# Half of the first sixteen modulation vectors by TensorE, transposed tokens in four PSUM banks in turn

## The reference

```
mod = silu(c) @ w_mod + b_mod              # 6 * 1024 numbers
sh1, sc1, g1, sh2, sc2, g2 = split(mod, 6)
u = layer_norm(x) * (1 + sc1) + sh1        # 512 x 1024
z = u @ w_in                               # q, k, v, f, ca, cb, ga, gb
...
```

## Time and profile before

| | us |
|---|---|
| median of three executions | 1709.74 |
| the profiled execution, whole | 1707.66 |
| its span in the profile | 1705.8 |
| TensorE (PE) busy | 1616.3 (95%) |
| VectorE (DVE) busy | 1320.6 (77%) |
| ScalarE (ACT) busy | 689.8 (40%) |
| start of tile(3) on TensorE | 53.19 |

### The profile page before, as it was taken

One profiled execution on the slowest core, in us unless ns is written; L12 is line 12 of the kernel. 1 busy time (PEld: TensorE's weight loads), 2 busy tenths in 40 slices (PEclk: granted clock), 3 DMA queues, 4 the chain that ended last, 5 costly groups with the idle time before them and its releaser, 6 DMA issues.

```text
span 1705.8 us, 23135 instructions
## 1 busy us (share of the span) xinstructions
PE 1616.3 (95%) x8238; PEld 1372.2 (80%) x8238; DVE 1320.6 (77%) x2726; ACT 689.8 (40%) x1036; POOL 657.5 (39%) x450
## 2 busy tenths in 40 slices
PE   3999999994999999999998999999989999999996
PEld 3887777774899999999997998998966677676775
DVE  7479776888489899979957988988965555556689
ACT  3334565424334345545453343343233333333332
POOL 2000000002035778687744743844714432332311
PEclk9999999997999999999999999999999999999999
DMA  7423224462676657577789988988979999999962
GB/s 271 167 82 124 87 99 163 148 208 76 238 259 200 174 163 186 156 220 175 209 246 349 371 331 319 390 318 328 327 259 381 404 361 356 341 383 366 351 238 81
DMA packets 181682, 422.29 MB, mean 248 GB/s; under 512 B 33600, under 2 KB 66496, under 8 KB 181568
## 3 DMA queue, kind: packets, MB, share of 16 engines
q1 hardware_dynamic: 91472, 264.44, 43.6%
q0 software_dynamic: 57200, 139.58, 24.2%
q10 hardware_dynamic: 32896, 16.78, 3.5%
HBM read 375.55 MB, written 45.15 MB: 247 GB/s over the span
## 4 chain that ended last, share of the span: by engine, by line
PE 72%; DVE 20%; DMA 4%; ACT 2%; issue 2%; DVEq 0%; POOL 0%; SPq 0%; ACTq 0%; POOLq 0%
PE bank L1686 21%; PE bank L1687 21%; PE bank L1688 21%; PE bank L1965 3%; DVE one L1474 2%; DVE wlo L1306 2%; DVE one L1472 2%; DVE one L1476 2%; DMA gates_by_key<-stage 1%; DVE raw L996 1%; DMA vraw<-in_v_tab_dram 1%; PE bank L1914 1%; PE bank L1779 1%; PE bank L1764 1%; DVE stats L1007 1%
## 5 line engine op out<-in xcount | busy, mean ns | idle before, releaser
L1686 PE MATMUL bank<-act_hi,whi 128*128 128x384 f32 (+1 forms) x1352 | 482.1, 357 | 11.6 <-ACT gelz L872 4.3
L1687 PE MATMUL bank<-act_lo,whi 128*128 128x384 f32 (+1 forms) x1352 | 473.4, 350 | 0.0
L1688 PE MATMUL bank<-act_hi,wlo 128*128 128x384 f32 (+1 forms) x1352 | 473.3, 350 | 0.0
L1686 PE MATMUL bank<-vhi,eh 128*128 128x512 f32 x768 | 304.7, 397 | 8.8 <-DVE vlo L1514 8.8
L1687 PE MATMUL bank<-vlo,eh 128*128 128x512 f32 x768 | 301.2, 392 | 0.0
L1688 PE MATMUL bank<-vhi,el 128*128 128x512 f32 x768 | 300.5, 391 | 0.0
L1686 PEld LDWEIGHTS bank<-act_hi,whi 128*128 128x128 f32 x1352 | 256.3, 190 | 28.6 <-issue 9.2
L1514 DVE TENSOR_TENSOR vlo<-vraw,vhi 128x512 fp32r<-128x512 f32 x256 | 176.3, 698 | 126.4 <-ACT vhi L925 125.7
L1687 PEld LDWEIGHTS bank<-act_lo,whi 128*128 128x128 f32 x1352 | 256.2, 190 | 14.3
L1688 PEld LDWEIGHTS bank<-act_hi,wlo 128*128 128x128 f32 x1352 | 255.8, 189 | 13.3
L662 POOL DMA_INDIRECT gates_by_key<-selW,selS x128 | 237.9, 1859 | 68.2 <-issue 46.6
(11 more groups left out here) (235 smaller groups left out, 1993.6 us busy)
## 6 DMA issues: line engine op xcount, KB each, us to landing
raw<-in_u_t_dram SPq DMA_DIRECT2D x128, 512.0 KB, 6.3
vraw<-in_v_tab_dram SPq DMA_DIRECT2D x256, 256.0 KB, 6.3
raw<-in_wblk_dram SPq DMA_DIRECT2D x61, 512.0 KB, 4.1
raw<-in_w_modt_dram SPq DMA_DIRECT2D x48, 512.0 KB, 4.0
gring<-gates_by_key SPq DMA_DIRECT2D x32, 768.0 KB, 8.5
gates_by_key<-stage ACTq DMA_DIRECT2D x8, 2048.0 KB, 11.4
gelu_ahead<-gelz SPq DMA_DIRECT2D x20, 768.0 KB, 4.2
gback<-gelu_ahead SPq DMA_DIRECT2D x40, 384.0 KB, 6.9
```

The costliest lines, as they stand in the source:

```text
L1686: mm(o, wh, mh, start=start, stop=False)
L1687: mm(o, wh, ml, start=False, stop=False)
L1688: return mm(o, wl, mh, start=False, stop=stop)
```

## The change

The eight slices are split. The vectors of slices 0, 3, 6 and 7 (`DOTTED`) stay dots on VectorE, from buffers of their own, `early_w` (two blocks, 1 MB, each). Those of slices 1, 2 and of 4, 5 (`BY_ROWS`) are made by TensorE, four vectors at a time, by a relay:

1. `mod_rows`: eight float32 matmuls with 32 equal columns of silu(c) (`cwide`) as the weights and 512 columns of w_mod in its natural layout (`modn`, 2 MB for each relay) as the moving side. The four 32-column strips of the array take four of the eight input tiles each pass, and leave four partial sums in four groups of partitions of bank 7.
2. `rows_out`: VectorE copies bank 7 (128 x 512) to `mrows`.
3. `mod_columns`: four float32 matmuls, weights a 128 x 128 piece of mrows, moving side one column `strips` that has a 1 in each strip: they add the four partial sums and turn the row into columns.
4. `turned_in`: VectorE adds the bias (128 x 4) and counts `mod_r` up by two.

The transposed tokens now use banks 3 to 6 in turn: slices 0 to 3 at once, slices 4 to 7 by `late_turn` (four transposes each) when ScalarE has read the bank. TensorE therefore has the nine products, the late transposes and the relays in one written order. Weight blocks 0 to 2 are loaded before the modulation, and the ring starts with them; the order of SyncE's loads is cside, cs, the four token tiles, early_w 0, four small ones, blocks 0 to 2, modn 0, early_w 1, modn 1, early_w 2, early_w 3, block 3 and so on. Several of the new buffers lie where hc, qa and ka lie later, so POOL's memsets of those three now come when all sixteen vectors are there.

```
@@ load order, SyncE @@
+            sp.dma_start(cside[:], ccol).then_inc(c_in, 16)
             sp.dma_start(cs[:], cb.broadcast_to([P, D])).then_inc(c_in, 16)
-            for s in range(RAW):
-                sp.dma_start(raw[:, s, :], w_modt[STREAM[s][1]]).then_inc(raw_in[s], 16)
-                sp.dma_start(xres[:, s, :], x[s * P:(s + 1) * P, :]).then_inc(x_in[s], 16)
+            for t in range(TT):
+                sp.dma_start(xres[:, t, :], x[t * P:(t + 1) * P, :]).then_inc(x_in[t], 16)
...
+            load_early(0)
             for dst, src in ((bmod[:], b_modc), (bf[:], b_fc), (convw[:], conv_wc), (convv[:], conv_vec)):
                 sp.dma_start(dst, src).then_inc(small_in, 16)
+            for n in range(FIRST):
+                sp.dma_start(raw[:, n, :], wblk[n]).then_inc(raw_in[n], 16)
+            load_natural(0)
+            load_early(1)
+            load_natural(1)
+            load_early(2)
+            load_early(3)
@@ VectorE @@
+            def early(i, j):
+                m = DOTTED[i] + KD * j
+                dve.wait_ge(early_in[i], 16)
+                return nc.vector.scalar_tensor_tensor(out=early_w[i][:, j, :], in0=early_w[i][:, j, :], scalar=1.0,
+                                                      in1=cs[:], op0=ALU.mult, op1=ALU.mult,
+                                                      accum_out=modc[:, m:m + 1])
+            def rows_out(i):
+                dve.wait_ge(rows_mm, i + 1)
+                nc.vector.tensor_copy(mrows[:], bank[7][:, :]).then_inc(rows_sb, 1)
+            def turned_in(i):
+                kd = BY_ROWS[i][0]
+                dve.wait_ge(turned, i + 1)
...
+                nc.vector.tensor_tensor(four[0][:, :, kd:kd + 2], four[2], four[1][:, :, kd:kd + 2],
+                                        ALU.add).then_inc(mod_r, 2)
...
+            early(0, 0)
+            with_bias(0, early(0, 1))
+            until(0)
+            low_part(0, 0)
+            until(FIRST - 1)
+            rows_out(0)
+            turned_in(0)
+            early(1, 0)
+            low_part(1, 0)
+            with_bias(3, early(1, 1))
+            low_part(2, 0)
+            low_part(3, 0)
+            rows_out(1)
+            turned_in(1)
+            early(2, 0)
+            low_part(4, 0)
+            with_bias(6, early(2, 1))
+            low_part(5, 0)
+            early(3, 0)
+            low_part(6, 0)
+            with_bias(7, early(3, 1))
+            low_part(7, 0)
@@ TensorE @@
+            def first_products(kd):
+                pe.wait_ge(a_lo, kd + 1)
+                for n in range(FIRST):
+                    if kd == 0:
+                        low_ready(n)
...
+            def late_turn(kd):
+                pe.wait_ge(u_raw, kd - 3)
+                turn(kd, range(TT), bank[FIRST + kd % 4])
+            def mod_rows(i):
+                if i:
+                    pe.wait_ge(mod_r, BY_ROWS[i - 1][1] + 1)
+                pe.wait_ge(modn_in[i], 16)
+                for pair in range(0, KD, 4):
+                    for j in range(4):
+                        last = mm(bank[7][j * QUAD:(j + 1) * QUAD, :], cwide[:, pair + j, :], modn[i][:, pair + j, :],
+                                  start=pair == 0, stop=pair == KD - 4)
+                last.then_inc(rows_mm, 1)
+            def mod_columns(i):
+                pe.wait_ge(rows_sb, i + 1)
+                for j in range(4):
+                    last = mm(bank[7][:, j:j + 1], mrows[:, j * P:(j + 1) * P], strips[:], start=True, stop=True)
+                last.then_inc(turned, 1)
...
+            first_products(0)
+            mod_rows(0)
+            late_turn(4)
+            mod_columns(0)
+            first_products(1)
+            late_turn(5)
+            first_products(2)
+            late_turn(6)
+            mod_rows(1)
+            first_products(3)
+            mod_columns(1)
+            late_turn(7)
+            for kd in range(4, KD):
+                first_products(kd)
```

More of the change, by code:

```diff
@@ L39 @@
 SPL = 3
[L42 to L45, removed]
+FIRST = 3
+DOTTED = (0, 3, 6, 7)
+BY_ROWS = ((1, 2), (4, 5))
+STREAM = []
+for _n in range(NBLK):
     STREAM.append(("w", _n))
@@ L170, in build @@
         cs = sb("cs", [P, D], F32, 197)
+        modn = [sb(f"modn{i}", [P, KD, HALF], F32, 88 + 16 * i) for i in range(len(BY_ROWS))]
+        early_w = [sb(f"early_w{i}", [P, 2, D], F32, at) for i, at in enumerate((181, 189, 120, 128))]
+        cwide = sb("cwide", [P, KD, QUAD], F32, 136)
+        cside = sb("cside", [P, KD], F32, 137)
+        strips = sb("strips", [P, 1], F32, 137.5)
+        mrows = sb("mrows", [P, HALF], F32, 179)
         rbc = sb("rbc", [P, 4, T], F32, 189)
@@ L1062, in _ @@
                 last = bn(xres, t, 1)
-            scales(last, 1, entry)
+            dve.wait_ge(cs_r, 2)
+            scales(last, 1)
             scaled(xn, xres, 0)
@@ L1688, in three, with turn, transposes @@
                 return mm(o, wl, mh, start=False, stop=stop)
-            def transposes(again):
+            def turn(kd, ts, into):
+                for t in ts:
+                    last = nc.tensor.transpose(into[:, t * P:(t + 1) * P], xn[:, t, kd * P:(kd + 1) * P], ident[:])
+                if ts[-1] == TT - 1:
+                    last.then_inc(xT_mm, 1)
+            def transposes():
                 for ts in ((0, 1), (2, 3)):
                     for t in ts:
-                        if not again:
-                            pe.wait_ge(*((xn_r, 1) if t < 2 else (xa_r, t - 1)))
-                        elif t % 2 == 0:
+                        if t % 2 == 0:
                             pe.wait_ge(xn_r, t // 2 + 2)
@@ L1699, in transposes @@
                     for kd in range(KD):
[L1700 to L1704, removed]
+                        turn(kd, ts, bank[kd])
             def low_ready(n):
@@ L1748, in rows_block @@
                 last.then_inc(blk_mm, blocks)
-            pe.wait_ge(const_r, 1)
-            transposes(False)
-            side_by_side(0, 3, 0, 3)
-            for n in range(3, G0):
+            def first_products(kd):
+                pe.wait_ge(a_lo, kd + 1)
+                for n in range(FIRST):
+                    if kd == 0:
+                        low_ready(n)
+                    w = slice(kd * P, (kd + 1) * P)
+                    high, low = w_parts(n)
+                    last = three(bank[n][:, :], high[:, w], low[:, w], act_hi[:, kd, :], act_lo[:, kd, :],
+                                 kd == 0, kd == KD - 1)
+                    if kd == KD - 1:
+                        last.then_inc(blk_mm, 1)
@@ L1754, in _ @@
+            first_products(0)
[12 more added lines that the diff above has]
+                first_products(kd)
+            for n in range(FIRST, G0):
                 if V0 <= n < F0:
@@ L1857, in _ @@
                     pe.wait_ge(g_row, 1)
[L1858 removed]
+            transposes()
             side_by_side(W0, 2, 2 * KD, KD + 2)
```

72 lines of the change are left out of this document (47 added, 25 removed).

## The result

| | before | after |
|---|---|---|
| median of 18 executions each, same chip | 1709.63 | 1712.36 |
| ratio, 95% interval | | 1.0016, 1.0009 to 1.0023 |
| the profiled execution, whole | 1707.66 | 1712.76 |
| its span | 1705.8 | 1710.9 |
| start of tile(3) on TensorE | 53.19 | 57.20 |

The account below looks back on a forecast made before the run. TensorE, busy 95%, passes on early delays; VectorE bounds the stage before tile(3). Higher-clock sum +0.5 plus clock falls 3.2 gave +3.7: 1707.66 to 1711.4, plus 2.08 for the median, 1713.4; range 1709.0 to 1717.0.

Parts of the forecast that it names:

- the gain at the tokens: Start of the stage: with the new order of loads, tokens normalised at 14.3 against 22.30 before, 8 us earlier.
- the relay's size: First relay, slice 0's products to the sum: rows 1.92 us, copy 0.69, columns 1.07; from 25.0 to 29.3.
- where the second relay comes: In TensorE's written order, rows behind slice 2's products, columns behind slice 3's; VectorE adds the bias at 42.1.
- Rival 2: Saved VectorE time counts in full if the second sum is ready at about 35.5: stage ends 47.1, -6.1 us; chance 0.09.
- the clock: TensorE's granted clock falls in the idle gaps at both relays, costing 3.2 us together (between 0 and 7).
- slice 0: Clock term: slice 0's products on TensorE at the lower clock cost 0.6 us.
- The first rows: Clock term: the first relay's rows run partly at the lower clock, costing 0.5 us.
- The first fall: Clock fall after the first relay costs 1.7 us, all on the chain, as slices 1 to 3 precede the second columns.
- the second fall: Clock fall at the second relay costs 0.4 us, since VectorE paces slices 4 to 7 and TensorE can catch up.
- Rival 3: Clock low through most of the stage, slices 1 to 3 at 3.8 us each: +7.5, 1717.2; chance 0.08 with rival 4.
- The rule of the Trainium skill: Copying out of PSUM costs 0.69 us per relay with TensorE waiting; with both copies hidden, 1.4 us less, 1712.0.
- The delay at tile(3): End of the stage: tile(3) starts 3.7 us later, at 56.9 instead of 53.19.

Follow-up runs that it names:

- the control: The changed kernel run again unaltered, in the same rounds as a one-relay version: 1711.84 (before 1709.05), ratio 1.0015, tile(3) at 56.46.
- The dots-ahead run: The changed kernel with the four dots of slices 6 and 7 moved ahead of VectorE's second copy: 1712.77 (before 1708.6), ratio 1.0018.
- the gaps filled: The changed kernel with products of zero weights added in TensorE's two gaps: 1710.85 (before 1708.6), ratio 1.0013, tile(3) at 54.09.
- dots alone: The changed kernel without relays, all sixteen vectors dots, new load order and four banks kept: 1706.09 (before 1708.6), ratio 0.9983, tile(3) at 49.37.

## Where the prediction was right and wrong

**Right: the gain at the tokens, the relay's size, where the second relay comes.** Tokens at 14.3, as said. The first relay takes 3.9 us from the rows' start to the sum's (25.45 to 29.34), 4.1 to 4.3 predicted; eight column instructions took 1.05 and 0.95 us where the float32 transposes of the earlier trace rows had given 1.07, and the strips 1.92 as in the earlier trace rows. No load was late. The written order of TensorE holds the second relay back, as Rival 2 has it turned round, and moving the rows ahead of slice 1's products turned the sign of the result (1703.72 and 1704.91 beside 1708.6 and 1708.9). Everything behind the stage passes the delay on.

**Right in sum, by two terms that were off and cancel: the clock.** The falls came where they were forecast, behind both relays. Of the 3.2 us: slice 0 was put at 0.6 and took 0.45 (rows at 25.45 instead of 25.0). The first rows, put at 0.5, ran at the higher clock. The first fall was put at 1.7 and cost 1.6: slice 1 takes 3.71 us (31.76 to 35.47) instead of 2.1. With the relays 0.3 to 0.4 us shorter each, the second sum came at 43.60, 1.2 us before the time that the prediction gives it with its terms for the clock (42.1 + 2.8, less 0.1 for the sum itself); in the control it came at 44.18, 0.6 us before that time.

**The step that failed**, under a total that came out near, is "the second fall 0.4, since VectorE paces slices 4 to 7 and leaves TensorE time to catch up". VectorE's own part was right: from the second sum to the end of the last low part 9.5 us were said, and 43.60 to 53.1 are 9.5. But TensorE did not catch up. Its slice 4 took 4.01 us (46.01 to 50.02) and slice 5 3.08, and with no gap up to 57.20 it reached tile(3) 2.0 us after 53.1 + 2.05 = 55.2, where the last low part alone would have allowed it. That term is 2.0, not 0.4. In the control it is 0.7: there eight products of slice 4 ran at the lower clock instead of fourteen, and tile(3) came at 56.46, where VectorE's last low part (end 53.7) would have allowed 55.8. The dots-ahead run shows it from the other side: low parts 2.8 us earlier, no earlier end. A sum that lets one engine pace a stage has to carry the other engine's line too, at the clock that it will have. From the second sum to tile(3) VectorE's line is 9.5 + 2.05 = 11.6 us. TensorE's is 2.4 until slice 4 can start (43.60 to 46.01) and 36 products at 0.23, 8.3: 10.7, and VectorE would pace, as it does with the gaps filled (11.8 measured). But fourteen at the lower clock (46.01 to 52.15) add 0.2 each, and 13.5 is more than 11.6.

**Rival 2's price was too high.** It is the same omission. With the sum at 35.77 (second execution of that kernel; 35.5 in the rival) the stage ended at 49.24, not 47.1, because TensorE then has 17 us of its own work. So 4.0 us are gained there and not 6.1. (Rival 3's terms, 0.5 + 5.3 + 2, add up to 7.8 and not to its 7.5.)

**The rule of the Trainium skill.** The earlier trace rows gives the length of a copy, 0.69 us; it does not show TensorE waiting for it, as the prediction has it. The changed kernel's trace has the first copy from 27.44 to 28.13, beside four transposes of slice 4 (27.30, 0.66 long), and TensorE waits 0.23 us for `mrows`. The second ran from 40.50 to 41.2 while slice 3's products filled TensorE until 42.54, and nothing waited for it. The Trainium skill, TensorEngine Tiling (Array Packing), Performance Considerations, says that emptying PSUM can become the bottleneck; in this trace it does not, and the 1.4 us that the prediction gave to this rule should have been about 0.2. By its own timeline the second copy had products beside it, and by the written order the first had transposes.

**The whole is near by luck as well.** The delay at tile(3) was put at 3.7 and was 4.0 in one profile and 3.3 in the control. The profiled execution was put at 1711.4 and took 1712.76, and its median was put 2.08 above it and lies 0.4 below: two misses that cancel in part. The execution of before that was profiled was a short one, 2 us under its median. From tile(3) to the end of the span it takes 1652.6 us, where the ten profiles of this case have 1652.3 to 1654.9; the changed kernel has 1653.7 and 1653.1. A prediction made from one profile of before inherits that execution's luck, in the stage and later. Why the medians show 0.5 to 1.3 us less than the stage is not settled; this scatter is large enough for it.

## What to carry to other kernels

Handing work to an engine that looks idle in a stage costs the waits of the exchange more than its instructions: here 9.5 us of dots were bought with 12.35 us of VectorE's waiting, and the stage grew by 7.1 to 7.8 us against dots alone. Place each half of such an exchange in the in-order queues so that the other engine has independent work until the answer is there; one exchange that is covered beat two that are not, with more work left on the "slow" engine, and moving the second ahead of slice 1's products won most of it back too. When the sum names one engine as the pace-maker, write down the other engine's line too, and test a change's parts apart: the new load order alone was a gain that the relays hid.

## What was not expected of the hardware

The clock falls mostly at the same places of the program in the ten traces; what differs is how long, and at some places whether. Read in windows of 1 us and counted from tile(3), there are stretches of lower clock from about 336, 858, 877 and 1209 us on in all ten profiles, and from about 775 in eight of them. That one lies in 820 to 836 us. Before, the changed kernel, and the control, which is the changed kernel again:

```profile
820.00:836.00 16.00, 13.95 (x80) 13.63 (x79) 15.83 (x25) 6.15 (x7) 11.11 (x6) 0.89 0.51 117
```

```profile
820.00:836.00 16.00, 13.96 (x92) 13.64 (x91) 15.79 (x42) 7.74 (x10) 12.49 (x8) 1.00 0.65 148
```

```profile
820.00:836.00 16.00, 14.01 (x80) 13.69 (x80) 15.80 (x42) 7.39 (x9) 12.47 (x8) 0.89 0.64 144
```

Not every such fall costs the same. Without this one the changed kernel came only 0.3 us nearer to the kernel before (the products with `one` at 827.31 and 830.86, 3.55 apart; at 870.40 and 873.61, 3.21): VectorE is busy for 15.8 of these 16 us, so it probably paces the place. The fall that starts at 930 is over by 933.4 before, and in the changed kernel it lasts into the window 936.8 to 940.2 (mean clock 0.58); there the distance grows by 1.2 us, from 3.33 (930.37 and 933.70) to 4.57 (936.12 and 940.69).

In the stage itself one kernel stood on both sides: with 0.81 us of waiting ahead of the second rows the clock stayed at its higher level in one execution, and with 1.40 us it fell in another. The wait was not all that differed: in the first slice 0's products had run at the lower clock (0.43 apart from 22.61 on), in the second at the higher, so which of the two decided is open. A profile of one execution therefore prices the falls of the clock only to within one or two us, which is as much as this case's result.
